# One decoder step on one core: the state chain's order of work, its first inverse on TensorE, and products issued in pairs

## What is computed

```python
proj = x_ext @ w_in                       # 1024 -> 12 attention tiles and 15 tiles for RWKV
att = dilated_window_attention(q, k, v)   # 8 heads, windows (128,1) (512,4) (2048,16), ALiBi
# RWKV-7, 8 heads of 64, per token:
sa = S @ (-kk_t)
S = S * w_t + outer(sa, kk_t * a_t) + outer(v_t, k_t);  y_t = S @ r_t
y_rw = (group_norm(y) + bonus) * g
x1 = layer_norm(ALPHA * x + concat(att, y_rw) @ w_out)
f = (silu(causal_conv3(x1 @ w_gate)) * (x1 @ w_up)) @ w_ffn_out
y = layer_norm(ALPHA * x1 + f)
```

## Time and profile before

| what | us |
|---|---|
| median of 3 runs (lowest, highest) | 914.76 (914.44, 915.19) |
| the profiled execution | 915.74 |
| its span, from first to last instruction | 913.9 |
| PE busy in the span | 827.9 |
| DVE, ACT, POOL busy | 518.0, 328.6, 259.4 |
| mean granted clock of TensorE | 0.964 |

### The profile page before, as it was taken

The page is one execution under the profiler, slowest core; times in us unless marked ns, Lnnn a source line. Parts: engine busy times, 40 slices in busy tenths (PEclk is TensorE's granted clock), DMA queues, the critical chain, the costliest instruction groups (busy, mean ns, idle before and its releaser), DMA issues.

```text
span 913.9 us, 22939 instructions
## 1 busy us (share of the span) xinstructions
PE 827.9 (91%) x9916; PEld 774.7 (85%) x9916; DVE 518.0 (57%) x772; ACT 328.6 (36%) x568; POOL 259.4 (28%) x113
## 2 busy tenths in 40 slices
PE   5999999998766668799997799999999999999994
PEld 5899888887546567678887699999999999999994
DVE  5478766685566866635644467766666663000036
ACT  5544455553220212224326444333333332111124
POOL 0000000001342535023424245544444444444300
PEclk9999999999987888999998899999999999999997
DMA  7232222242522221640212033333232332222302
GB/s 253 81 94 70 72 92 70 80 167 56 130 82 89 83 84 38 199 154 25 76 56 78 18 114 93 96 113 92 93 93 88 87 90 92 85 87 87 98 2 94
DMA packets 31301, 83.45 MB, mean 91 GB/s; under 512 B 5128, under 2 KB 8392, under 8 KB 30688
## 3 DMA queue, kind: packets, MB, share of 16 engines
q1 hardware_dynamic: 30048, 79.82, 28.4%
q10 hardware_dynamic: 1152, 2.16, 0.6%
HBM read 75.87 MB, written 5.91 MB: 89 GB/s over the span
## 4 chain that ended last, share of the span: by engine, by line
PE 83%; DVE 10%; ACT 4%; issue 2%; POOL 1%; ACTq 0%; DVEq 0%; POOLq 0%
PE banks L1772 81%; DVE xx L1181 2%; DVE sscore L1416 1%; PE banks L1826 1%; ACT x_hi L1089 1%; ACT z L1092 1%; DVE rw L1181 1%; PE banks L2154 1%; DVE z L1181 1%; DVE lower L1181 1%; DVE z L1184 1%; DVE ms L1181 1%; DVE ssa L1446 1%; ACTq L783 0%; ACT z L1152 0%
## 5 line engine op out<-in xcount | busy, mean ns | idle before, releaser
L1772 PE MATMUL banks<-x_hi,w_hi 128*128 128x264 f32 (+1 forms) x784 | 208.3, 299 | 16.2 <-DVE x_lo L1181 13.4
L1772 PE MATMUL banks<-x_hi,w_lo 128*128 128x264 f32 (+1 forms) x784 | 198.5, 286 | 0.0
L1772 PE MATMUL banks<-x_lo,w_hi 128*128 128x264 f32 (+1 forms) x784 | 198.5, 286 | 0.0
L1772 PEld LDWEIGHTS banks<-x_hi,w_hi 128*128 128x128 f32 x784 | 138.8, 191 | 29.4 <-issue 15.2
L664 POOL TENSOR_TENSOR w_lo<-w_raw,w_hi 128x1024 fp32r<-128x1024 f32 (+1 forms) x40 | 95.7, 2394 | 170.6 <-ACT w_hi L778 170.3
L1772 PEld LDWEIGHTS banks<-x_lo,w_hi 128*128 128x128 f32 x784 | 139.4, 192 | 0.1
L1772 PEld LDWEIGHTS banks<-x_hi,w_lo 128*128 128x128 f32 x784 | 139.2, 191 | 0.0
L664 POOL TENSOR_TENSOR wx_lo<-w_raw,wx_hi 128x1024 fp32r<-128x1024 f32 (+1 forms) x36 | 86.1, 2392 | 100.7 <-ACT wx_hi L778 100.2
L1184 DVE SCALAR_TENSOR_TENSOR z<-z,banks 128x260 f32<-128x260 f32 (+1 forms) x24 | 12.4, 515 | 118.6 <-PE banks L1772 112.1
L1772 PE MATMUL banks<-xx,lower 64*64 64x64 f32 x1280 | 56.1, 237 | 25.5 <-DVE xx L1181 19.1
L1772 PEld LDWEIGHTS banks<-xx,lower 64*64 64x64 f32 x1280 | 48.1, 148 | 36.0 <-DVE xx L1181 23.0
(11 more groups left out here) (253 smaller groups left out, 1710.8 us busy)
## 6 DMA issues: line engine op xcount, KB each, us to landing
w_raw<-in_w SPq DMA_DIRECT2D x87, 512.0 KB, 3.6
w_raw<-in_w SPq DMA_DIRECT2D x16, 448.0 KB, 3.2
kv<-in_ck SPq DMA_DIRECT2D x16, 192.0 KB, 3.3
kv<-in_cv SPq DMA_DIRECT2D x16, 192.0 KB, 3.4
att<-in_x ACTq DMA_DIRECT2D x8, 264.0 KB, 7.3
att_out<-att SPq DMA_DIRECT2D x1, 2112.0 KB, 9.3
z<-in_xc SPq DMA_DIRECT2D x1, 2080.0 KB, 7.9
y_out<-z SPq DMA_DIRECT2D x8, 260.0 KB, 2.2
```

The costliest lines, as they stand in the source:

```text
L1772: return pe.matmul(out, l, r, start=start, stop=stop)
```

## The change

1. The inputs `x` come through SP in eight pieces, first all of the first 264 columns, and ACT issues no DMA ahead of its first work; a dummy activation comes first on ACT. PE's second half waits for its own pieces only.
2. At the end of the projection DVE makes `mix_lo(CC - 1)` first; the last `shift` and the `gath` copies come after the first masks.
3. DVE's `xx` = identity - `lower` is gone. The mask carries the minus sign, and PE adds the identity by itself: per group four 64x64 by 256 identity products, two 256-column products and eight 64-column ones in place of eight of 64 columns. `x0_copy` copies two banks instead of one.
4. The products of `value_side` are issued one by one between those of `half_products` of level 1, those of `solved` between those of level 2, with all their waits ahead of the level.
5. The `vt_rows` transposes, `s_score`, the softmax steps, `decode_back`, `decode_values` and `own_heads` sit in other levels. POOL makes the first two state steps after three rows' `products`, not after eight.
6. SP loads `values_of(2)` and the later ones behind the state's output, `yrow` and the first late weights. `z` comes in two parts, each after its own transposes.
7. ACT's `late_high(0)`, `late_high(1)` come before block 3's token copies; `attn_out` takes two tiles' first halves, then their second halves.

```diff
 # SP
+        for half in range(2):
+            for q in range(KT // 2):
+                x = slice(half * XH, (half + 1) * XH)
+                sp.dma_start(att[:, 2 * q:2 * q + 2, x], a["x"][:, 2 * q:2 * q + 2, x])\
+                    .then_inc(x_landed[4 * half + q], 16)
         weights(1)
...
-        for v in range(4):
-            values_of(v)
+        values_of(0)
+        values_of(1)
         sp.wait_ge(sw_a, 6)
...
-        values_of(4)
         sp.wait_ge(sw_y, 1)
...
         weights(N_IN)
         weights(N_IN + 1)
-        values_of(5)
-        sp.wait_ge(bt_ps, 3 * TB)
-        sp.dma_start(z[:, :, :], a["xc"]).then_inc(z_landed, 16)
+        for v in range(2, 6):
+            values_of(v)
+        sp.wait_ge(bt_ps, 3 * TB - 2)
+        sp.dma_start(z[:, 0:CC, :], a["xc"][:, 0:CC, :]).then_inc(z_landed, 16)
+        sp.wait_ge(bt_ps, 3 * TB - 1)
+        sp.dma_start(z[:, CC:KT, :], a["xc"][:, CC:KT, :]).then_inc(zb_landed, 16)
 # POOL
-        for b in range(B):
+        for b in range(NKV):
             products(b)
...
         step(swk, swk, keys(1), ALU.mult)
+        for b in range(NKV, B):
+            products(b)
         pool.wait_ge(sw_sa, 1)
 # ACT, block 3
+                if n == TB - 1:
+                    late_high(0)
+                    late_high(1)
             token_copy(n)
 # DVE
-            link(tt(lower[:, hs, :, :]..., causal[:, 2 * CH:4 * CH]..., ALU.mult))
-            tt(xx[:, hs, 1, :], eye..., lower[:, hs, 1, :], ALU.subtract).then_inc(xt_done, 1)
+            tt(lower[:, hs, :, :]..., causal[:, 2 * CH:4 * CH]..., ALU.mult).then_inc(xt_done, 1)
...
-        ve.wait_ge(a_mix_hi, CC)
+        mix_lo(CC - 1)
         ve.wait_ge(ends_done, 1)
         inverse_start(0, 0)
         inverse_start(0, 1)
+        shift(N_IN - 1)
         key_masks(0)
+        for q, src in (...):
+            ve.tensor_copy(gath[:, :, q, :], ...).then_inc(ga_done, 1)
...
-                if n == 0 and l >= 4:
-                    s_score(l - 4)
+                if (n, l) == (0, 5):
+                    s_score(0)
                 if n == 1:
-                    s_score(l + 1)
+                    s_score(l)
                 if (n, l) == (2, 1):
-                    s_score(B - 1)
-                if (n, l) == (2, 2):
+                    state_sum(0)
+                if n == 2 and l in (2, 3):
+                    s_score(l + 4)
+                if (n, l) == (2, 4):
                     s_shifted()
-                    state_sum(0)
-                if (n, l) == (2, 3):
-                    s_scaled()
...
+                if (n, l) == (2, 4):
+                    s_scaled()
 # PE
         def start_inverse(n, g):
             pe.wait_ge(xt_done, 2 * n + g + 1)
-            for i in range(4):
-                for j in range(2):
-                    ins = mm(banks[rows(1 - j), 4 * g, i * CH:(i + 1) * CH], xx[rows(j), 4 * g + i, 1, :],
-                             level[rows(j), NLEV, :])
+            o = slice(0, 4 * CH)
+            for j in range(2):
+                eye = level[rows(j), NLEV, :]
+                for a in range(2):
+                    mm(banks[rows(j ^ 1 ^ a), 4 * g + a, o], eye, eye.unsqueeze(1).broadcast_to([CH, 4, CH]), True, False)
+            for j in range(2):
+                eye = level[rows(j), NLEV, :]
+                mm(banks[rows(j), 4 * g + 1, o], eye, lower[rows(j), 4 * g:4 * g + 4, 1, :], False, True)
+                for i in range(4):
+                    ins = mm(banks[rows(1 - j), 4 * g, i * CH:(i + 1) * CH], lower[rows(j), 4 * g + i, 1, :], eye,
+                             False, i == 3)
...
-                half_products(n, l)
-                if n >= 1 and l <= 3:
-                    (value_side, solved, step_terms)[l - 1](n - 1)
+                if n >= 1 and l == 1:
+                    value_waits(n - 1)
+                    half_products(n, l, lambda h, j: value_side(n - 1, h, j))
+                elif n >= 1 and l == 2:
+                    solved_waits(n - 1)
+                    half_products(n, l, lambda h, j: solved(n - 1, h, j))
...
-                if (n, l) in ((0, 2), (0, 3)):
-                    vt_rows(l)
-                if (n, l) == (2, 5):
-                    decode_values(0)
-                if n == 3 and l != 3:
-                    decode_values((1, 2, 0, 3, 4)[l - 1])
+                    vt_rows(1)
+                if (n, l) == (0, 2):
+                    vt_rows(2)
+                    vt_rows(3)
+                if n == 3 and l <= 3:
+                    decode_values(l - 1)
+                if (n, l) == (3, 5):
+                    decode_values(3)
...
+        value_waits(TB - 1)
+        ...
+        decode_values(4)
+        attn_out(0)
+        solved_waits(TB - 1)
+        ...
+        decode_values(5)
+        attn_out(1)
```

## The result

The changed kernel takes **906.24 us** (median of 18 runs, 901.63 to 911.72), beside 915.71 us for the kernel before in the same session (median of 18, 909.66 to 919.43). The ratio is 0.9913, interval 0.9897 to 0.9929: faster by 0.9%. The forecast was 895.5 with a range of 883 to 905. The sign was right; the size was half of what was forecast, and the measured time lies 1.2 us above the range.

The account below looks back on a forecast made before the run. The projection was taken as PE-bound, the chain as paced by the PE-DVE loop of products, masks and updates, plus clock loss. Terms summed to -19.3 us from 915.74, giving 896.4, or 895.5 at the median, range 883 to 905.

Parts of the forecast that it names:

- first half products: Chain's start: no gath copies, xx operations or one vt_rows ahead of the first half products, -1.7 us.
- block 0: Block 0: vt_rows done by level 2, so level 3 waits less, and one score sum leaves, -5.0 us.
- block 0 to 1: End of block 0 to block 1's first half products: DVE's subtraction, stretched by POOL, is removed, -3.5 us.
- block 1 to 2: End of block 1 to block 2: stretched subtraction removed, -4.15, less 0.85 for new identity products, -3.3 us.
- block 2 to 3: End of block 2 to block 3: no stretch to remove, only the new identity work is left, +0.7 us.
- block 3: Block 3: interleaving, moved decode_values and a stall give -3.5, the late value load in level 3 costs +7.5, net +4.0 us.
- behind the chain: Stretch behind the chain: PE idle and a value step go, two decode_values of about 1.0 us each come, -0.4 us.
- everything behind 409 us: Everything behind 409 us is untouched by the change and left as it is, 0 us.
- rival 2: Interleaved and identity products run one after the other, or DVE hides them: 903 us, chance 0.12.
- rival 3: POOL or SP becomes late, s_score(3) waits behind POOL's early state steps: up to 5 us, 901 us, chance 0.08.
- Rival 4: Slower: longer PE stands lower the clock, now in block 3 too, where it adds up to 28 us: 922 us, chance 0.03.
- The first rival: Value load isn't waited for, or clock stays at 2.4 GHz in blocks 1 and 2: -7 to -12, 886 us, chance 0.25.

Follow-up runs that it names:

- early values: Kernel after, with the value load for block 3's third value product issued ahead of the wait for the state sum: 895.32 us, ratio 0.9785 to the kernel before.
- the start alone: Kernel before, with only SP issuing the x loads in eight parts and ACT loading its table first: 912.13 us, ratio 0.996.
- the alternation alone: Kernel before, with only value-side and solve products issued one by one between half products in levels 1 and 2: 910.39 us, ratio 0.9944.
- values before weights: Kernel after, with the value load still behind the state sum and state row but ahead of the two late weights: 903.27 us, ratio 0.9875.
- the three parts in the old order: Kernel before, with new start, TensorE first inverse and alternating products together; decode levels, SP order and order behind the chain unchanged: 906.12 us, ratio 0.9893.
- early sums: Kernel after, with the value load ahead of the state sum's wait and decode sums ahead of the gate and last step terms: 893.97 us, ratio 0.9774.
- the run undone: Kernel after, with value-side and solve products issued whole behind the half products again: 911.61 us, ratio 0.9949.
- The three built on it: On the 893.97 us kernel: block 0's first inverse by DVE (894.9 us), one decode value product put back into the chain (895.17), both (894.93).

## Why the prediction was half right

The terms of the sum, as forecast and as the two profiled executions have them. Blocks are cut where the forecast cut them, at the first half products and at the first mask of `inverse_start` (before 260.53, 310.60, 357.46; after 251.87, 293.61, 334.57). Both traces are single executions.

| term | forecast | measured |
|---|---|---|
| start | -2.4 | -2.75 |
| entry | -1.2 | -0.9 |
| first half products | -1.7 | +0.3 |
| block 0 | -5.0 | -5.3 |
| block 0 to 1 | -3.5 | -2.7 |
| block 1 | -3.0 | -5.6 |
| block 1 to 2 | -3.3 | -2.7 |
| block 2 | -3.5 | -3.2 |
| block 2 to 3 | +0.7 | +2.0 |
| block 3 | +4.0 | +7.4 |
| behind the chain | -0.4 | +2.5 |
| everything behind 409 us | 0 | +2.5 |
| sum | -19.3 | -8.5 |

**Right.** The start, block 0, the step that removes the stretched subtraction, the alternation and that a wait for the value load appears in level 3 of block 3. Up to the start of block 3 the sum was -22.9 by forecast and -20.9 by trace.

**The value load: right mechanism, wrong size.** The step that failed is "behind 1 MB of weights lands at S + 8.1 (3.2 after its issue) to S + 9.6", and with it the wait of 4.5 to 6 us. The load landed at S + 12.8, and the wait was 9.23. The run without the weights ahead of it lands at S + 8.2, so S + 8.1 is the time of the load alone: SP took 3.13 us to issue the four parts, not the 1.7 that I took, and the last landed 3.6 behind its issue. With the weights ahead the last part left at S + 5.9, not S + 4.9, and landed 6.9 behind its issue, not 3.2 to 4.7, while the DMAs moved 260 GB/s, where I had taken 300. Of the 4.6 us between the two runs, 1.3 lie in SP's issues and 3.3 between issue and landing. For block 3 that makes: without the wait (early values) it is 2.0 us shorter than in the kernel before, where the forecast's other parts (-3.5, and 1.0 for the step) make -2.5; the wait and its clock are 9.35 together (41.28 less 31.93), not 6.5. So 2.9 of the 3.4 us by which block 3 was off are the load's. The forecast had read the danger and taken too cheap a price for it, since it added the four steps of one queue as if each were at its best.

**The first inverse: the price was taken from the wrong side.** I priced PE's products at 0.85 us against 0.5 and left them out of the term "first half products" altogether. They cost 1.0 us at each start: 5.84 against 6.85 us at the chain's start, 5.4 against 6.5 between blocks 2 and 3. That would make up the 0.8 and 0.6 us by which "block 0 to 1" and "1 to 2" are short. Of the 2.0 at "2 to 3" 1.1 go with the inverse (6.5 against 5.4), and 0.9 stay without it (5.4 against 4.55), for which no run shows the cause. The stretch removed is 3.0 and 4.15 in the one execution that I had; with the start alone and with the alternation alone, where the subtraction is the same, it was stretched by 1.9 us behind block 0 (2.35 less 0.43), so even this gain isn't a constant. The first term was off by 2.0, and 1.5 of that is the clock: the kernel after ran its first scores at the lower level in the profiled execution (1.99 us for 64 records), others of the same code at the full one (1.16 for 64), and there the first half products came 6.8 us behind the chain's start instead of 8.3.

**Behind the chain.** PE's idle time in the stretch fell from 1.81 us to 0.74 (length less busy, in the windows), not to 0; the two value products are 2.1; "0.7 of a value step" lay ahead of the stretch and gave nothing in it. That makes +1.0, and the other 1.5 is the clock, 0.91 on 18 us where it had been 1.00. The trace of values before weights splits it in the same way: to `gsq` 17.4 us in the kernel before, 18.4 there at clock 1.00, 19.9 in the kernel after. What the step left out is the new order's own wait: the sums stand behind the gate and the step terms, and PE waits 0.73 us for them. Whether the clock's 1.5 belongs to the new order is open: four of its five traces with that wait have such a fall, but so have two of the five with the old order (17.80 and 17.54 us up to `centre`, beside 16.25).

**Everything behind 409 us.** "I leave it as it is" was wrong by 2.5 us, with no instruction changed. From ACT's `gsq` to the end it is 500.6 us in the kernel before and 503.15 after. The difference lies in the 50 us across the layer norm and the FFN's start (the last windows of the result): PE's idle time is within 0.6 us the same, and the clock is 0.80 instead of 0.86. The other traces tie this neither to the change nor to the moment at which the chain ends. The clock there is 0.86, and the time from `gsq` to the end 500.7 to 501.0 us, with the start alone, the alternation alone and early values, whose chain ends 26 us earlier than in the kernel before. It is 0.80, and that time 502.9 to 503.7, with the three parts in the old order, values before weights and early sums. So this term is a difference between executions as far as the record goes; what decides it is open.

**The rivals.** Serialised products (rival 2) are refuted by the alternation alone, clear of nothing, and by the records of the trace; the run undone agrees. POOL (rival 3) was not late: PE's wait for `sscore` in blocks 0 to 2 fell from 2.1 to 1.0 us. Rival 4 had the right place, the clock in block 3, but of its 28 us some 2 came (4.0 us of PE work in the window at 0.50). The first rival didn't come: the load was waited for, and the clock was 0.86 and 0.88 in blocks 1 and 2. Taking the forecast's 6.5 us for wait and clock out of the sum gives 889, and the run with early values, where both are gone, got to 895.3. Its trace (890.7 us of span, 23.2 less than before, where the sum would have 25.8) lacks the most behind the chain: 2.5 us longer there, where the forecast had 0.4 shorter. Most of the rest is that this trace is 2.8 us faster than its kernel's median.

**The best kernel** by its median is the one with early values and early sums, 893.97 us, ratio 0.9774 to the kernel before: 2.3% where the change itself gave 0.9%. The three built on it (0.9771 to 0.9779), and early values alone (0.9785), can't be told apart from it.

## What to carry to other kernels

When an edit moves a load behind a wait, write down the queue from the wait to the landing: every issue at the longest duration of its kind, every transfer ahead of it at full length. Ask of each statement between them whether it needs to be there; here one that didn't cost more than the whole change had won. An operation that is moved to a free engine has its price at every place, also where the old one never suffered, so take the gain at the places with a collision and the cost at all of them. And leave some us of the range for the stretches that the edit doesn't touch, and don't look for a cause there before several traces agree: here the same instructions took 500.6 to 503.8 us in fourteen traces, by the clock that they were granted.

## What the runs showed that was not expected

- 64 records of half and value-side products took 1.33 us alternating, 0.9 us less than apart, with both row tiles writing both banks.
- PE's stalls for its own instructions changed from kernel to kernel with no edit near them: 2.9 us in blocks 0 to 2 of the kernel after, 10.2 and 10.1 from 260 to 375 us in the two with block 0's inverse on DVE, the longest single one 4.2 us.
- With the subtraction gone, the lock between POOL and DVE caught a copy of the same kind: 3.02 us in the kernel before with TensorE's inverse and 2.95 with the three parts together, beside 2.02, 1.97 and 1.17 with the subtraction (before, start alone, alternation alone), and 1.32 in the kernel after.
- 1 MB of weights ahead of a value load moved its landing by 4.6 us, from S + 8.2 to S + 12.8.
- The same wait of 0.73 us was followed by 4 us at clock 0.57 in the kernel after, and by products at 1.00 in the one with the values ahead of the weights.
- The clock across the layer norm and the FFN's start was 0.80, 0.83 or 0.86 on the same instructions, and the time to the end went with it (502.9 to 503.8, 502.0 to 503.1, 500.6 to 501.0 us).
